# Normalising the x blocks first, rotating one projection late, splitting a norm by column halves and moving the pair sums to GpSimd in a two-layer diffusion backbone

## The reference

```
q = (h @ wq).reshape(t, 8, 2, 128)                      # per head, two halves
s = einsum('thpd,hpnd->thpn', q, sub_keys)              # 128 scores per half
sv, si = top_k(s, 16)
cand_s = sv[:, :, 0, :, None] + sv[:, :, 1, None, :]    # sums of pairs
best_s, best = top_k(cand_s, 16)                        # 16 experts of 16384
act = gelu(h @ u[idx]);  out = sum(softmax(best_s) * act * v[idx])
```

## Time and profile before

| | |
|---|---|
| Median of 3 runs | 2792.86 us (2791.81 to 2797.53) |
| The profiled execution | 2791.21 us, its span 2789.3 us |
| TensorE matmul busy | 2615.5 us (94% of the span) |
| VectorE busy | 2291.9 us (82%) |
| ScalarE busy | 1157.5 us (41%) |
| GpSimd busy | 853.9 us (31%) |
| PEER ranking and early scores, layer one | from 507.7 to 702.0 us of the span |
| From layer one's last expert to layer two's attention scores | 1782.8 to 1875 us |
| Layer two's output projection, norm, first query | 1954.5 to 2001.6 us |
| PEER ranking and early scores, layer two | 2015.2 to 2136.0 us |

### The profile page before, as it was taken

The page is one execution under the profiler, slowest core; times in us unless marked ns, Lnnn a source line. Parts: engine busy times, 40 slices in busy tenths (PEclk is TensorE's granted clock), DMA queues, the critical chain, the costliest instruction groups (busy, mean ns, idle before and its releaser), DMA issues. The chain is left out here.

```text
span 2789.3 us, 41396 instructions
## 1 busy us (share of the span) xinstructions
PE 2615.5 (94%) x14062; PEld 2262.2 (81%) x14062; DVE 2291.9 (82%) x4353; ACT 1157.5 (41%) x1916; POOL 853.9 (31%) x570
## 2 busy tenths in 40 slices
PE   7999999998889999999999999799898779999997
PEld 4788865888778899999999999665598658988886
DVE  5888885999878788888887888845498779999999
ACT  5333333332653333333333333315344546666664
POOL 0000001444663344443333333200367532222221
PEclk9999999999899999999999999899899999999999
DMA  6313233134699999998888888420334999999996
GB/s 268 121 76 135 96 116 125 64 127 146 181 301 394 330 335 338 334 338 317 309 311 306 311 308 312 180 113 1 136 127 155 323 361 354 362 353 361 359 363 238
DMA packets 247819, 682.39 MB, mean 245 GB/s; under 512 B 20172, under 2 KB 106804, under 8 KB 244020
## 3 DMA queue, kind: packets, MB, share of 16 engines
q1 hardware_dynamic: 192436, 480.00, 47.6%
q0 software_dynamic: 55296, 201.35, 20.1%
HBM read 635.34 MB, written 45.92 MB: 244 GB/s over the span
## 5 line engine op out<-in xcount | busy, mean ns | idle before, releaser
L1231 PE MATMUL bank<-v_parts,p_parts 128*128 128x512 f32 x3072 | 743.4, 392 | 8.7 <-DVE p_parts L2284 8.7
L1231 PEld LDWEIGHTS bank<-v_parts,p_parts 128*128 128x128 f32 x3072 | 578.1, 189 | 127.0 <-issue 8.9
L1171 PE MATMUL bank<-h_parts,u_hi 128*128 128x384 f32 (+1 forms) x2048 | 512.0, 333 | 13.5 <-POOL u_lo L2566 8.3
L1171 PEld LDWEIGHTS bank<-h_parts,u_hi 128*128 128x128 f32 x2048 | 372.4, 191 | 22.7 <-issue 12.8
L2282 DVE TENSOR_TENSOR v_parts<-arena,v_parts 128x1024 fp32r<-128x1024 f32 x256 | 313.4, 1224 | 48.5 <-ACT v_parts L1662 48.2
L1171 PE MATMUL bank<-h_parts,u_lo 128*128 128x384 f32 (+1 forms) x1024 | 340.9, 333 | 0.0
L1662 ACT ACTIVATE v_parts<-arena 128x1024 fp32r<-128x1024 f32 x256 | 269.1, 1051 | 78.4 <-PE bank L1231 52.7
L2585 POOL DMA_INDIRECT arena<-in_v,arena x128 | 196.4, 1535 | 321.5 <-DVE arena L2304 297.6
L1659 ACT ACTIVATE arena<-bank 128x384 f32<-128x384 f32 x104 | 50.9, 490 | 555.3 <-PE bank L1171 555.3
L2255 DVE TENSOR_TENSOR u_lo<-arena,u_hi 128x1024 fp32r<-128x1024 f32 x208 | 253.4, 1218 | 18.1 <-ACT u_hi L1569 16.1
L2585 POOL DMA_INDIRECT arena<-in_ug,arena x128 | 178.2, 1392 | 265.0 <-DVE arena L2297 240.3
(11 more groups left out here) (346 smaller groups left out, 4652.9 us busy)
## 6 DMA issues: line engine op xcount, KB each, us to landing
arena<-in_u SPq DMA_DIRECT2D x256, 512.0 KB, 5.5
arena<-in_v SPq DMA_DIRECT2D x256, 512.0 KB, 5.6
arena<-in_wm SPq DMA_DIRECT2D x80, 512.0 KB, 5.1
arena<-in_wst SPq DMA_DIRECT2D x19, 2048.0 KB, 8.0
gate_scratch<-arena SPq DMA_DIRECT2D x18, 2048.0 KB, 8.7
arena<-gate_scratch SPq DMA_DIRECT2D x30, 768.0 KB, 7.7
arena<-in_whd SPq DMA_DIRECT2D x8, 2560.0 KB, 9.4
arena<-gate_scratch SPq DMA_DIRECT2D x30, 384.0 KB, 6.6
```

Source lines behind the costliest of these rows:

```text
L1171: last = mm(banks[q][:, 0:ND[p]], w[:, q, col], h[:, k, DS[p]], start=(n3 == 0), stop=(n3 == 3 * KT - 1))
L1231: last = mm(banks[2 + 2 * b + half][:, :], x[:, q, at:at + P], y[:, q, col], start=(first and i == 0), stop=(final and i == 2))
```

## The change

It has five parts.

1. **x first.** `norms(1, ...)` takes the blocks in the order 2, 3, 0, 1. The gate products of block 0 (from `y_tok`) come ahead of the wait for TensorE's last result. ScalarE normalises and modulates x first; the context blocks are turned in `turn_step` calls between projections 1 to 4, and modulated between the copies. VectorE's `back` for blocks 2 and 3, which stood ahead of the projections, stands behind rotary steps 3 and 5, and a fold of modulation columns behind step 6. `rtmp` gets another place.
2. **Deferred rotations.** `project(n)` is issued before `rotate(n - 1)`; `rotate(9)` stands behind the first block's values. Rotation 0 also waits for all four variances (`ln_v`, 8), because it writes into banks that the norm reads.
3. **A norm by column halves.** The output projection of layer two runs in the order (block 2, half 0), (3, 0), (2, 1), (3, 1), and `half_front` does products, sum and statistics of a half as soon as it is there.
4. **High part on VectorE.** In layer two ScalarE only modulates, and VectorE makes the high part (a copy) ahead of the low part, as it already does for x in layer one. GpSimd handles the two variances between its first three low parts of weights instead of ahead of them.
5. **Pair sums on GpSimd, one group later.** The four sums of a block (a "set") are issued by GpSimd (`pairs`), between its low parts of query weights and of early experts, at places written out in `PAIRED_EARLY`. They wait for `ranked` (the last `top16` stage of that block). VectorE ranks the next group's blocks first and then the sums of the group before, for which it waits (`paired`).

The core of the diff:

```diff
+        ranked, paired, RANKED = hw_h, hw_l, [5 * HEADS, 5 * HEADS + 4 * NB]
+        cand_odd = ar(B_M, 512, c=NB, h=2, n=NCAND)
+        PAIRED_EARLY = [[8, 8, 9, 10, 12, 13, 14, 15, 16], [2, 3, 3, 4, 5, 5, 6, 7, 8]]
-        WOUT_ORDER = [[...], [(0, 1), (0, 0), (1, 0), (1, 1)]]
+        WOUT_ORDER = [[...], [(0, 0), (1, 0), (0, 1), (1, 1)]]
-        rtmp = ar(A_C1 + 2048, 1024, s=2, t=512)
+        rtmp = ar(A_OT + 2048, 1024, s=2, t=512)
...
-            turn_normalised(4, [0, 1], hT_done, KT, xT_pe)
+            turn_normalised(4, [1], hT_done, KT, xT_pe)
+            def project(n):
+                if n % 4 == 0:
+                    arrived("qkv", n // 4)
+                if n >= 2:
+                    pe.wait_ge(qk_sb, n - 1)
+                if n == 8:
+                    pe.wait_ge(hT_done, 3 * KT)
...
+            def rotate(n):
+                pe.wait_ge(qk_sb, n + 1)
+                if n == 0:
+                    pe.wait_ge(swa_c, 48)
+                    pe.wait_ge(ln_v, 8)
+                if n >= 2:
+                    pe.wait_ge(rope, n - 1)
...
+            project(0)
+            for n in range(1, 10):
+                project(n)
+                rotate(n - 1)
+                if n <= 4:
+                    for k in range(2 * n - 2, 2 * n):
+                        turn_step(4, 1, 0, k, hT_done, KT, xT_pe)
...
 # ScalarE
-                    for k in range(KT + 1):
-                        if k < KT:
-                            act.wait_ge(x1T, 2 * KT + k + 1)
-                            modulate(1, k, 1, hf, 3, h1)
-                        if k:
-                            act.wait_ge(h1, H1_BASE[1] + k)
-                            af_(h_hi[:, k - 1, TS[1]], hf[:, k - 1, TS[1]], ACT.Copy).then_inc(hh, 1)
+                    for k in range(KT):
+                        act.wait_ge(x1T, 2 * KT + k + 1)
+                        modulate(1, k, 1, hf, 3, h1)
...
+                if 1 <= i <= 4:
+                    for k in range(2 * i - 2, 2 * i):
+                        act.wait_ge(xT_pe, 2 * KT + k + 1)
+                        modulate(1, k, 0, hT, 0, hT_done)
...
 # VectorE
+                def half_front(i, b, half):
+                    cols = slice(512 * half, 512 * half + 512)
+                    dve.wait_ge(y_pe, y_need[i][half])
+                    products(i, b, half)
+                    st_.wait()
+                    link(V.scalar_tensor_tensor(ln_x[:, b, cols], ln_x[:, b, cols], ALPHA, ln_t[:, i % 4, cols], ALU.mult, ALU.add))
+                    did(V.bn_stats(stat[:, i * 20 + 6 * half:i * 20 + 6 * half + 6], ln_x[:, b, cols]))
...
+                if call == 1:
+                    for half in range(2):
+                        products(2, blocks[2], half)
+                    dve.wait_ge(y_ac[1], 1 + PAIRS)
+                    for i in range(2):
+                        front(i, blocks[i])
+                    sums(2, blocks[2])
+                    front(3, blocks[3])
+                    return finish_rows
...
+                def best_pairs(i):
+                    dve.wait_ge(paired, RANKED[p] + nb * (i + 1))
+                    top16([(bs[:, b, 2 * i + h, :], biu[:, b, 2 * i + h, :], pair_sums(p, i, b)[:, h, :])
+                           for b in blocks for h in range(2)])
                 for i in range(4):
                     for n, b in enumerate(blocks):
                         dve.wait_ge(ps_sb, PS_BASE[p] + nb * i + n + 1)
-                        top16([(sv[:, b, m, :], siu[:, b, m, :], sc[:, b, m, :]) for m in range(4 * i, 4 * i + 4)])
-                        svh = ...
-                        for at, a0, na, w in PAIR_SETS:
-                            did(V.tensor_tensor(cand[:, b, :, at:at + na * w]...))
-                    st_.wait()
-                    top16([(bs[:, b, 2 * i + h, :], biu[:, b, 2 * i + h, :], cand[:, b, h, :]) ...])
+                        top16([(sv[:, b, m, :], siu[:, b, m, :], sc[:, b, m, :]) for m in range(4 * i, 4 * i + 4)], ranked)
+                    if i:
+                        best_pairs(i - 1)
+                dve.wait_ge(ranked, RANKED[p] + 4 * nb)
+                best_pairs(3)
...
+                if i in (3, 5):
+                    ln1([i // 2 - 1])
+                if i == 6:
+                    fold(1, 3, lncol1, [1])
...
 # GpSimd
+                def pairs(x):
+                    i, b = x // nb, blocks[x % nb]
+                    pool.wait_ge(ranked, RANKED[p] + x + 1)
+                    if p == 0 and x == nb:
+                        pool.wait_ge(tok_done, 1)
+                    svh = sv[:, b, 4 * i:4 * i + 4, :].rearrange("p (h c) k -> p h c k", c=2)
+                    for at, a0, na, w in PAIR_SETS:
+                        last = G.tensor_tensor(pair_sums(p, i, b)[:, :, at:at + na * w]..., ALU.add)
+                    last.then_inc(paired, 1)
...
+                        if p and i == 0 and 1 <= m <= 2:
+                            norms(8, [m - 1])
                         pool.wait_ge(qw_h, 16 * p + 4 * i + m + 1)
                         hi, lo = weight_parts(m)
                         G.tensor_tensor(lo, w[:, :, m * P:(m + 1) * P], hi, ALU.subtract).then_inc(qw_l, 1)
+                        if p == 0 and 4 * i + m >= 11:
+                            pairs(4 * i + m - 11)
+                        if p and i == 3 and m % 2:
+                            pairs(m // 2)
+                x = [5, 2][p]
                 for j in range(KA[p]):
...
                     G.tensor_tensor(lo[:, q, :], raw[:, q, :], hi[:, q, :], ALU.subtract).then_inc(u_l[q], 1)
+                    while j < len(PAIRED_EARLY[p]) and x < PAIRED_EARLY[p][j]:
+                        pairs(x)
+                        x += 1
```

More of the change, by code:

```diff
@@ L1987, in front, with sums @@
                     for half in range(2):
[L1988 to L1989 removed]
+                        products(i, b, half)
+                    sums(i, b)
+                def sums(i, b):
+                    st = stat[:, (i % 4) * 20:(i % 4) * 20 + 20]
                     if call == 0:
@@ L2020, in norms @@
                         between()
-                def finish_rows(some):
-                    for i in some:
-                        back(i, blocks[i])
                 return finish_rows
```

123 lines of the change are left out of this document (61 added, 62 removed).

## The result

The changed kernel takes 2754.92 us (median of four runs, 2753.82 to 2760.26) beside 2792.34 for the kernel before (2790.69 to 2797.53). The ratio is 0.9867, with a 95% interval of 0.9848 to 0.9885: 37.4 us faster. The profiled execution has a span of 2752.0 us instead of 2789.3. On the pages, TensorE is still busy for 94% of the span.

A forecast was written before the change was run, and what follows sets the result against it. TensorE, busy in 94% of the span, was taken as the bound. Terms 8.7 + 4.9 + 6.9 + 6.1 - 1.0 + 4.4 = 30.0 us off 2791.2 gave 2761.2, plus 1.65 for the median: 2762.9 us, range 2757 to 2776.

The forecast's parts named there:

- Pair sums, layer one: Early scores of layer one: additions moved to GpSimd end VectorE's ranking at 632.0 instead of 640.75; 8.7 us gained.
- Pair sums, layer two: Early scores of layer two: the ranking ends at 2090.0 instead of 2093.89, VectorE ends last; 4.9 us gained.
- The rule decides: Rival, both layers' rankings: slower GpSimd additions lie on the path, 12 us lost instead of 13.6 gained, 2788; chance 0.05.
- Dear sets: Rival, both layers' rankings: a set costs 2.4 us on GpSimd, gaining 2.7 - 0.5 instead of 13.6, 2774; chance 0.12.
- Slower: Rival, both layers' rankings: VectorE blocks GpSimd's additions, a set costs 4.8 us, 2815 in all; chance 0.05.
- Contention given back: Rival, VectorE's work behind the ranking: two more instructions wait for a whole low part, 4.7 us, 2767.4; chance 0.13.
- x first: Between layer one's experts and projection 0: the first x turn comes at 1794.1 instead of 1800.97; 6.9 us gained.
- Deferred rotations: Projections ahead of attention: ten gaps of 0.8 us vanish, 16 context transposes of 0.11 come in; 6.1 us gained.
- TensorE's clock: At projection 0: longer idling ahead puts more of it at 1.2 GHz; between 0 and 2.3 us lost, taken as -1.0.
- Layer two's norm and first query: Behind layer two's output units: first turn 1.85 us earlier, fewer waits for low parts in the first unit; 4.4 us gained.
- the first unit's 24 products at 1.2 GHz need 5.1: Layer two's first query unit: 24 x 0.213 = 5.1 of its 7.2 us are products, 2.1 were waits for low parts.

The follow-up runs named there:

- the doubled sets: The changed kernel with the four additions of every set on GpSimd done twice, the first time into unused room: 2767.46 us, ratio 0.9917.

## Why the prediction was right and where it was wrong

The direction and the places held, and most of the mechanism: wrong were the base of the sum, the clock in two terms, and which engine ends last in layer two. The time fell below the range.

- **Pair sums, layer one, 8.7.** The trace has 10.6, the kernel with the sums put back 10.3, but against the second trace of before it is 6.9. The chain ran as I wrote it: the sums of group 1 were ready 80.28 us behind the first scores, where I had 80.8; from there to the ranking's end it was 42.96 us instead of 43.5. Together these are 1.1. The rest, 0.8, is VectorE's work behind the ranking, 60.4 instead of 61.2. TensorE's wait there was 4.1 us, not 6, because VectorE ended 1.9 us earlier than forecast; TensorE arrived 179.6 us behind the first scores, which is where the forecast had it. What I left out is that TensorE's arrival makes the larger part of the gain: it came 6.5 us earlier (186.1 before), with 3.7 us of gelu waits gone and a mean granted clock of 0.990 instead of 0.972, and the last wait gave 4.1.
- **Pair sums, layer two, 4.9.** 6.4, 4.6 and 4.6 in the three traces. That VectorE ends last, as I had it, was so only in the first (1.34 us of wait); in the others TensorE did, and what shrank is its gelu wait, 7.0 us before and 2.1 to 2.8 now. VectorE's waits for sets were in my list, for groups 0 and 1, but I took them as given and didn't ask whether the sets had to stand there: their rankings were done 29 us (layer one) and 17 us (layer two) before that low part.
- **The rule decides**, the Trainium skill's page "GPSIMD Engine Reference", section "Performance versus the Vector engine": by it elementwise sums should stay on VectorE, as GpSimd takes 1.96 times as long. Here a free set is 0.84 us on GpSimd and 0.50 on VectorE, 1.7 times as long, so the ratio roughly agrees; the conclusion drawn from it does not, as the blocked additions cost 19 to 26 us a layer. This rival falls, as do *Dear sets* and *Slower*. *Contention given back* didn't happen in the changed kernel (60.3 to 60.4 and 40.2 to 41.0 us behind the rankings, 58.7 to 61.2 and 40.0 to 41.1 before), but the doubled sets show it whole.
- **x first, 6.9.** 5.95 to projection 0, the missing 0.9 being a power instruction of GpSimd that was held up. With what the rounds take back it is 2.4 to 2.9 net; 1.75 of this return, the transposes, was in the forecast's next term.
- **Deferred rotations, 6.1, and TensorE's clock, -1.0.** Together 6.2, 5.0 and 5.2 against the first trace of before. The round is 4.33 us as forecast. The clock's loss isn't to be seen: in the first 4 us of projection 0 the granted clock was 0.77 and 0.50 in the two traces of before, and 0.79, 0.50 and 0.55 in those of the change. It scatters as much in one kernel as between them. Traces with like clocks give the forecast's 6.1: 68.1 to 61.9 at 0.77 and 0.79, 69.2 to 63.1 at 0.50.
- **Layer two's norm and first query, 4.4.** 5.9, 5.0 and 5.0. The way to the first turn became 1.85 shorter, of which the run with whole rows shows 1.80 for the halves, and the high part gave 0.47, as forecast. The step that failed is "the first unit's 24 products at 1.2 GHz need 5.1". They took 3.83 to 4.75, because the clock rose within the unit: groups of three products go from 0.64 to 0.36 us apart after the third group in the first trace. The term held the whole unit at the lower clock.

The step that put the time outside the range is the sum's base: it is made against one profiled execution, and all its other stretches are taken as fixed. Of the 7.3 us between the forecast and the span's gain of 37.3, 3.0 lie ahead of all changed code and are that execution's own. The terms that I mis-sized make 1.9 (layer one), 1.5 (layer two) and 1.5 (norm and first query), 1.1 more is the clock; what the other stretches took and gave, x first's 0.9 and attention's 1.0 among it, makes up the difference. The range reached 5.9 us below the forecast, from the bounds of costs alone, while executions of one kernel spread over 7 us and more (2783 to 2800 for before). The two later measurements, 2756.8 and 2756.4, lie below the range's end as well, by 0.2 and 0.6 us, which is less than the runs can tell.

That three terms were too small holds against the first trace of before. By the means of the two traces of before and the three of the changed kernel, the five stretches together gained 30.7 us, beside a forecast of 30.0. That this comes so near is in part luck: by the same means x first was forecast 0.9 us too high, and the rotations with the clock, and the first query, 0.9 too low each.

What stays open: by the traces, the means of the two and of the three executions are only 29.5 us apart, by the medians of the runs 33 to 37. The last stretch of the experts, which no edit touches, was 653 to 655 us in the two traces of before and 654 to 659 in the three of the changed kernel. In the thirteen variants it was 653.9 to 660.1, in seven of them 656.8 or more. I didn't find out whether that is scatter or a cost of the change.

## What to carry to other kernels

An instruction that is cheap when free and blocked by a neighbour is priced by where it falls: the same 32 additions cost VectorE 20 us in one arrangement and 26 in another, and GpSimd, which was the cause of the blocking, 7. When work goes to another engine, look where in that engine's order it stands: an idle stretch just ahead of work that is ready is a gain that costs a few moved lines (9.3 us here). And a sum of terms made from one execution needs a range at least as wide as two executions of the same kernel differ.

## What the runs showed of the hardware

- GpSimd's additions of 16, 32 and 48 elements a partition took 220, 244 and 270 ns, in all 96 cases undisturbed, beside VectorE's MAX8, MATCH_REPLACE8 and FIND_INDEX8, which weren't lengthened either.
- A copy of 128x256 on VectorE took 13.36 us instead of 1.4 while GpSimd ran six low parts without a pause. The Trainium skill, page "SBUF — State Buffer", section "Who interferes with whom", has it that when VectorE runs in a mode that takes both ports, which a copy can enter, whichever of VectorE and GpSimd issues first holds the shared ports for its whole instruction, and the other blocks. The trace agrees that it blocks; in which mode the copy ran, no row tells. But the copy didn't get its turn when the instruction in front of it ended; it came through in GpSimd's first pause.
- TensorE's granted clock was 0.50 in the first 24 query products of layer two before the change, with a wait of 1.49 us among them. It was 0.79, 0.61 and 0.62 in the three traces of the changed kernel, where no wait stands among them, 0.56 with high parts on ScalarE, and between 0.51 and 0.82 in the other variants. I tested no cause for this. The stretch of the first of the three, read as the earlier trace rows are:

```profile
1966.76:1970.59 3.83, 3.83 (x28) 3.83 (x27) 3.83 (x11) 0.95 (x2) 0.00 (x0) 0.79 0.89 364
```
